# Score banks of an attention stage: the two sample pairs put in different PSUM banks, and one prompt item fewer scored ahead of them

## The reference

```
s = (einsum('bqhd,bkhd->bhqk', q_nope, k_nope) + einsum('bqhr,bkr->bhqk', q_rope, k_rope)) * ATTN_SCALE
if mask is not None: s = where(mask, s, NEG_INF)      # prompt: block-causal, chunks of 64
p = softmax(s, axis=-1)
o = einsum('bhqk,bkhd->bqhd', p, v)
```

## Time and profile before

| | |
|---|---|
| Time, median of 3 runs | 1514.25 us (1514.23 to 1516.24) |
| Profiled execution: its time | 1514.12 us |
| Profiled execution: its span | 1512.3 us |
| TensorE matmul busy | 1485.5 us (98%), 10592 instructions |
| VectorE, ScalarE, GpSimd busy | 805.0, 618.8 and 697.0 us (53%, 41%, 46%) |
| Mean granted TensorE clock | 0.995 of full speed |
| DMA | 80 GB/s mean |

### The profile page before, as it was taken

How to read it: one execution, slowest core, us unless ns; L and a number is a source line. 1 busy time by engine, 2 the same in 40 slices (tenths; PEclk the granted TensorE clock), 3 DMA queues, 4 the chain that set the end, 5 groups by cost and what they waited for, 6 DMA issues and landing times.

```text
span 1512.3 us, 29016 instructions
## 1 busy us (share of the span) xinstructions
PE 1485.5 (98%) x10592; PEld 1406.6 (93%) x10592; DVE 805.0 (53%) x1397; ACT 618.8 (41%) x1236; POOL 697.0 (46%) x453
## 2 busy tenths in 40 slices
PE   9999999999999999999999999999999999999998
PEld 7789999999999999998987878787999999999998
DVE  6005716755645636547856464556456636456365
ACT  4413201123534434335448475656225434344342
POOL 7454454453363543634766061514243544635434
PEclk9999999999999999999999999999999999999999
DMA  7322232222132231321532010101122231412312
GB/s 231 89 82 82 67 111 83 62 77 70 57 128 69 84 101 48 128 84 55 163 112 74 2 56 1 55 0 55 42 70 57 84 118 50 137 57 83 111 55 90
DMA packets 36384, 120.32 MB, mean 80 GB/s; under 512 B 6040, under 2 KB 6744, under 8 KB 36064
## 3 DMA queue, kind: packets, MB, share of 16 engines
q1 hardware_dynamic: 30240, 109.20, 23.5%
q10 hardware_dynamic: 6080, 10.28, 2.2%
HBM read 115.91 MB, written 3.55 MB: 79 GB/s over the span
## 4 chain that ended last, share of the span: by engine, by line
PE 48%; ACT 2%; DVE 2%; issue 1%; ACTq 0%; DVEq 0%
PE ps L649 8%; PE ps L651 8%; PE ps L650 8%; PE ps L785 5%; PE ps L787 5%; PE ps L786 5%; PE ps L1040 2%; PE ps L1019 2%; PE ps L975 1%; PE ps L989 1%; PE ps L1048 1%; ACT kT L1894 1%; PE ps L978 1%; DVE neg_max L1541 1%; PE ps L954 1%
## 5 line engine op out<-in xcount | busy, mean ns | idle before, releaser
L649 PE MATMUL ps<-h_hi,w_hi 128*128 128x288 f32 x1280 | 380.6, 297 | 0.0
L650 PE MATMUL ps<-h_lo,w_hi 128*128 128x288 f32 x1280 | 377.5, 295 | 0.0
L651 PE MATMUL ps<-h_hi,w_lo 128*128 128x288 f32 x1280 | 376.3, 294 | 0.0
L590 POOL TENSOR_TENSOR w_lo<-raw,w_hi 128x512 fp32r<-128x512 f32 x128 | 173.5, 1365 | 220.7 <-ACT w_hi L1722 220.5
L785 PE MATMUL ps<-op_hi,w_hi 128*128 128x288 f32 x896 | 266.4, 297 | 4.4 <-DVE x L1338 4.3
L786 PE MATMUL ps<-op_lo,w_hi 128*128 128x288 f32 x896 | 265.0, 296 | 0.0
L787 PE MATMUL ps<-op_hi,w_lo 128*128 128x288 f32 x896 | 264.1, 295 | 0.0
L651 PEld LDWEIGHTS ps<-h_hi,w_lo 128*128 128x128 f32 x1280 | 241.1, 188 | 0.0
L649 PEld LDWEIGHTS ps<-h_hi,w_hi 128*128 128x128 f32 x1280 | 239.8, 187 | 1.2
L650 PEld LDWEIGHTS ps<-h_lo,w_hi 128*128 128x128 f32 x1280 | 240.3, 188 | 0.0
L581 POOL TENSOR_TENSOR w_lo<-raw,w_hi 128x1024 fp32r<-128x1024 f32 x60 | 145.2, 2425 | 183.9 <-ACT w_hi L1714 183.9
(11 more groups left out here) (200 smaller groups left out, 2755.5 us busy)
## 6 DMA issues: line engine op xcount, KB each, us to landing
raw<-stream SPq DMA_DIRECT2D x206, 512.0 KB, 3.6
out_x<-x ACTq DMA_DIRECT2D x8, 288.0 KB, 2.5
x<-xt SPq DMA_DIRECT2D x4, 288.0 KB, 5.9
x<-xt ACTq DMA_DIRECT2D x4, 288.0 KB, 9.1
raw<-stream ACTq DMA_DIRECT2D x2, 512.0 KB, 7.0
b_bc<-bs ACTq DMA_DIRECT2D x2, 512.0 KB, 6.6
cache_raw<-cache_ct ACTq DMA_DIRECT2D x1, 1024.0 KB, 5.5
v_out<-sgu_grow ACTq DMA_DIRECT2D x1, 512.0 KB, 4.9
```

Source lines behind the costliest of these rows:

```text
L590: nc.gpsimd.tensor_tensor(block_of(w_lo, b), factor(i, b), block_of(w_hi, b).bitcast(F32), ALU.subtract).then_inc(split_lo, 1)
L649: nc.tensor.matmul(out, l_hi, r_hi, start=first, stop=False)
L650: nc.tensor.matmul(out, l_hi, r_lo, start=False, stop=False)
L651: return nc.tensor.matmul(out, l_lo, r_hi, start=False, stop=last)
```

## The change

S0 moves to the last 64 columns of bank 2 and to banks 3 and 4; S1 stays where it was (bank 5 from column 448, 6, 7). The two no longer share a bank. Both now have the 64 new keys first and the 1024 cached ones behind. VectorE's wait ahead of the maximum of S1 is dropped. Each pair's small matmuls (last 64 keys) stand with its large ones, so that S0 is signalled before any small matmul of S1.

Since S0 needs bank 2, only P0 and P1 are scored ahead of the samples; P2 goes behind them. The order on TensorE becomes: key 10, P0, key 11, P1, key 12, samples, P2, P3, turn 0, turn 1, fill, P4, P5, turn 2, pv 0, P6, turn 3, and from there as before. On ScalarE it becomes P0, P1, S0, S1, turn 0, P2, P3, turn 2, P4, P5, turn 4, P6, P7, turn 6. The fill goes to bank 2 and waits for the exponential of S0. P2 takes bank 0 after P0, P3 bank 1 after P1, P4 bank 2 after S0, P5 bank 0 after P2.

```diff
-ITEMS = PROMPT[:3] + [("sample", 0, 0), ("sample", 1, 0)] + PROMPT[3:]
+ITEMS = PROMPT[:2] + [("sample", 0, 0), ("sample", 1, 0)] + PROMPT[2:]
-SAMPLE_ITEM = 3
+SAMPLE_ITEM = 2
...
-    steps = [("key", KT_N - 3), ("score", 0), ("score", 1), ("key", KT_N - 2), ("score", 2), ("key", KT_N - 1),
+    steps = [("key", KT_N - 3), ("score", 0), ("key", KT_N - 2), ("score", 1), ("key", KT_N - 1),
              ("samples", 0)]
-    first_ahead = [ITEMS.index(PROMPT[i]) for i in range(RING, 2 * RING)]
+    first_ahead = [ITEMS.index(PROMPT[i]) for i in range(RING - 1, 2 * RING - 1)]
...
-        if kind == "prompt" and 2 * RING <= ahead < len(PROMPT):
+        if kind == "prompt" and 2 * RING - 1 <= ahead < len(PROMPT):
...
-        if step[0] == "score" or step == ("gather", 0):
-            n = 1 if step[0] == "score" else 2
+        if step[0] in ("score", "samples") or step == ("gather", 0):
+            n = 2 if step[0] == "gather" else 1
...
+def probs_before(step):
+    kind, n = step
+    return (SAMPLE_ITEM if kind == "samples" else n) + 1
...
-            at = 3 * 512 if pair == 0 else 8 * 512 - SKEYS
+            at = (3 if pair == 0 else 6) * 512 - DEC
...
-            if pair == 0:
-                return kt * P
             return DEC + kt * P if kt < 8 else 0
...
-                    pe.wait_ge(probs_set, g * NI + (before[1] + 1))
+                    pe.wait_ge(probs_set, g * NI + probs_before(before))
...
-                        if pair == 0:
-                            for owner, hh in ((0, 0), (0, 1), (1, 0), (1, 1)):
-                                last = part(owner, hh, 8, DEC)
+                        for hh in range(2):
+                            last = part(pair, hh, 8, DEC)
                         last.then_inc(scored, 1)
...
                         row_max(SAMPLE_ITEM, sample_scores(0))
-                        dve.wait_ge(probs_set, g * NI + (SAMPLE_ITEM + 1))
                         row_max(SAMPLE_ITEM + 1, sample_scores(1))
```

## The result

The changed kernel takes 1517.38 us (median of 10 executions, 1514.91 to 1521.23), the kernel before 1514.24 (10 executions, 1510.39 to 1516.24). The ratio is 1.0025, with a 95% interval of 1.0016 to 1.0034: slower by 3.1 us, or 0.25%. The forecast was 1518.0 within 1514.4 to 1521.3. The profiled execution of the changed kernel took 1517.43 us, its span 1515.6 against 1512.3.

A forecast was written before the change was run, and what follows sets the result against it. TensorE, busy 98% of the span, bounds the kernel. From 1514.12 us, removing its one fall (2.5) gives 1511.6; four groups at -0.06 give 1511.4; two falls of 3.3 give 1518.0, range 1514.4 to 1521.3.

The forecast's parts named there:

- The dropped wait: VectorE's maximum of S1 no longer waits for S0's exponential: starts 0.11 us behind the samples, 0.94 us earlier.
- P2 behind the samples: P2's 0.65 us of TensorE work moves behind the samples, covered by old waits: P6 0.06 us earlier at full clock.
- The small term: Samples to P6 at full clock: 4.46 us of work against 4.52 now, so -0.06 us in each of four groups.
- The start of the samples: ScalarE's row of six key copies, and no order on TensorE, sets when the samples' matmuls start.
- The slack at P5: TensorE reaches P5 0.1 us behind P2's exponential, so no new wait; if wrong, up to 0.3 us a group.
- The cost of a fall: Samples at the low clock take 3.31 us longer; each fall costs 3.3 us, low bound 2.5.
- The number of falls: Groups of four whose clock falls at the samples: two 0.43, one 0.27, three or four 0.18, none or chain in full 0.12.
- The sign that the prediction named: More than one group shows its samples at 7.2 us and the clock at 0.50; one or none would refute it.
- the hole of 2.45 us in front of line 785: Single TensorE hole before 716.5 us; the clock fell 1.1 us behind it, taken as the neighbouring case.
- the upper bound of the interpolation: Behind a hole of 2.45 us every group falls; today's 1.41 us gives one of four; 2.06 us taken as two.
- a clock that changes at another place in each run: From the skill: the activity monitor runs freely, so the number of falling groups is a draw in every run.
- the clear steps: Run times would sit on one of several steps set by the number of falling groups, rather than between them.

The follow-up runs named there:

- the kernels with useful work in the holes: Changed kernel, S0 and S1 exchanging banks, S0's large matmuls issued early in the holes; two further versions move the fill, then ScalarE's order: 1510.98, 1507.08, 1505.49 us.
- the filled kernels: Dummy matmuls put in the holes ahead of the samples: changed kernel 1512.05 us, kernel before 1511.98; changed kernel with the wait also put back 1515.29.
- the old size of the hole: Changed kernel plus three dummy matmuls (0.66 us), bringing the hole ahead of the samples to its size in the kernel before: 1513.54 us, repeated 1513.10.
- the grown hole: Hole ahead of the samples at about 2 us: changed kernel profiled twice (1517.38, 1517.47 us) and changed kernel without the fill (1518.63).
- the first version with early sample matmuls: Changed kernel with S0 and S1 exchanging banks and S0's large matmuls issued in the holes, fill still behind turn 1: 1510.98 us, ratio 0.9980.

## Why the prediction was right

The dropped wait. Forecast: S1's maximum 0.11 us behind the end of the samples' matmuls and its exponential 0.94 us earlier. Measured: 0.11 and 0.96. Worth on the path: the prediction let it just pay for P2. That is what came out at full clock; with the wait put back, the new order is 3.24 us slower (3.3 was expected ahead of that run).

P2 behind the samples. Forecast: covered by the old waits, P6 0.06 us earlier a group at full clock. Measured, samples to P6: 8.38 in the first group and 8.39 in the third, against 8.31 and 8.39 in the first and the second before, so between 0.07 later and nothing. The small term had the wrong size, 0.2 to 0.3 us over four groups. The start of the samples did stay tied to ScalarE's row of copies.

The slack at P5 was put at 0.1 us. The kernel without the fill, in which P5 waits for the exponential, has P5 at 7.34 us, and the one with it at 7.38: a slack of 0.04, so the reading was right, and it is the reason that no new wait came.

The cost of a fall. Forecast: 3.3 us now that no wait gives any back. Measured: 3.2 in the second group. But the fourth group's fall covered only part of its samples (5.59 us, not 7.2), and cost 1.6. That a fall can be half a fall was not in the sum; the forecast took all at full price, and this, with 1.1 us of difference from the start of the program that no term foresaw, is how 1518.0 and 1517.4 met so closely. The agreement of the totals is better than that of the terms. Whether the longer low clock at the start is chance is not shown; it is in both profiles of the changed kernel, whose code there is that of the kernel before, and also in one of the kernels with useful work in the holes.

The number of falls. Forecast: two of four at 0.43. Measured: two of four in each of three profiles, the same two each time. The sign that the prediction named (more than one group with its samples at 7.2 us and the clock at 0.50) is met in part only: one group is so, the other is at 5.59 us and 0.69. That a larger hole costs more of the clock is shown by the filled kernels and the old size of the hole, not by this count. From the medians, 1517.4 less 1512.05 is 5.3 us that filling takes off the changed kernel (0.35% by the ratios, which allow for the chip), and 1513.98 less 1511.98 is 2.0 off the one before, beside it on the same chip. One argument behind the number was wrong: the hole of 2.45 us in front of line 785 was taken, from one trace, as one that always makes the clock fall. The changed kernel has the same hole and no fall behind it:

```profile
716.64 0.40 PE L789 MATMUL ps<-op_hi,w_hi 128*128 128x288 f32 x1 [2.45 <-DVE x L1341]
...
716.50:719.90 3.40, 3.26 (x24) 3.26 (x25) 3.02 (x7) 2.63 (x5) 0.86 (x1) 1.00 0.00 0
```

Of the twelve profiles at hand six fall there and six do not. So the upper bound of the interpolation was not "every group" but about one in two, and that two of four came out is partly luck. Of the six profiles without that fall, three are those with the grown hole: the falls of one execution are perhaps not independent of each other, and nothing here settles it.

The page of the Trainium skill ("TensorE: Matmul & The Clock Gate", "What's actually happening") was cited for a clock that changes at another place in each run. The times of ten executions of the changed kernel agree with it: 1514.91 us at a mean clock of 0.996, seven between 1516.29 and 1517.82 at 0.995 to 0.993, 1518.27 at 0.993 and 1521.23 at 0.992. The times do not sit on the clear steps that the prediction took from it, which partial falls would explain. The places agree with it less well: the low clock at 716 us is there in six profiles of twelve, but the three profiles with the grown hole have theirs in the same two groups.

What stays open, since no run tried it: at what place in the hole a fall begins, why one covers all of the samples' matmuls and another a part of them, and why it is the second and the fourth group.

## What to carry to other kernels

Moving work from ahead of a wait to behind it costs nothing by the chain of waits as long as the wait covers it, but it makes the hole ahead larger, and TensorE's clock pays for the hole afterwards: here 3 us for some 0.6 us more of idle time in each of four places. Where such a hole can't be closed, fill it, best with work that the next step needs, as soon as its operands and bank are there. And a filler belongs inside a wait: as soon as an edit shifts the wait in front of it, the filler itself is on the path, as the 1.34 us were in the first version with early sample matmuls.

## What the runs showed of the hardware

The clock fell with no single hole of TensorE longer than 0.99 us: 0.99 and 0.93 us with transposes and one score between them were enough in six groups of twelve (the same two in each of three profiles), 0.54 and 0.87 in one of twelve (two of these three profiles being of executions below their medians). Three dummy matmuls (0.66 us) that bring the former to the size of the latter took 4.4 us off the median. The same single hole of 2.45 us, at the same place of the program, was followed by the low clock in six executions of twelve. A spread of 6 us (0.4%) between executions of one kernel on one core came with the mean granted clock, between 0.992 and 0.996.
